# A decoder layer on one core: the three small slabs stored in order of the contraction, loaded and split in halves, with products of zeros on TensorE ahead of them

## The chip, the cores and the metric

The kernel runs on one core of one Trainium2 chip. The metric is the device time of one execution in microseconds (us). The core has five engines that run beside each other: TensorE (PE, matmuls; its weight loads are listed as PEld), VectorE (DVE), ScalarE (ACT), GpSimd (POOL) and SyncE (SP, here only the issuer of DMAs). They wait for each other through semaphores.

## The reference

One hybrid decoder layer on x of shape 256 x 2048 in float32. One input projection feeds 16 RWKV-7 heads and 8 heads of differential attention; an output projection, a layer norm, a squared-ReLU MLP (8192 wide) and a second layer norm follow.

```python
proj = x @ w_in[l]                     # 2048 x (3*1024 + 64 + 64 + 160 + 3*1024)
p = proj[..., :RWKV_COLS]
mixed = p + (_token_shift(p) - p) * mu # every column of the RWKV part
r, k, v, w_d, a_d, g_d = jnp.split(mixed, splits, axis=-1)
w = -jax.nn.softplus(-(w0 + jnp.tanh(w_d) @ w_up)) - 0.5
decay = jnp.exp(-jnp.exp(w))
a = jax.nn.sigmoid(a0 + a_d @ a_up)
g = jax.nn.sigmoid(g_d) @ g_up
...                                    # the scan over 256 steps, the attention
mix = jnp.concatenate([y_rwkv, y_diff], axis=-1) @ w_out[l]
x = _layer_norm(DEEPNORM_ALPHA * x + mix, ln1_gain[l], ln1_bias[l])
h = jnp.square(jax.nn.relu(x @ w_ff1[l])) @ w_ff2[l]
x = _layer_norm(DEEPNORM_ALPHA * x + h, ln2_gain[l], ln2_bias[l])
```

The change concerns the 288 small columns w_d, a_d and g_d of the first product, which need the most steps before anything else can use them: w_d (64 columns) and a_d (64) fill one accumulator of 128 columns, g_d (160) the next two, of which the second overlaps the first by 96 columns.

## The kernel before, in words

All weights reach the core in slabs of 128 partitions x 2048 float32 (1 MB). A slab lands in one of four `stage` buffers. ScalarE copies it to `whi` (rounded to fp32r), VectorE writes the rest, `stage - whi`, to `wlo`; there are two buffers of each. The activations are split in the same way into `acthi` and `actlo`. A product is then three fp32r matmuls: `whi*acthi`, `whi*actlo`, `wlo*acthi`, for each block of 128 columns (fb) and each block k of 128 of the 16 blocks of the contraction. The helper `mm` (L436) issues every matmul, so that nearly all TensorE rows have that line; they are told apart by their tiles. Likewise L1001 is every ScalarE operation, L1296 every full `wlo`, L1305 every `actlo`, L354 every slab's DMA.

The order of the work is written out by hand, in one program for each engine. The start goes as follows.

- SyncE issues x piece 0 (4 of 16 blocks, 512 KB), slab 0, x pieces 1 to 3, slab 1, two small vectors, slab 2, the weights `w_up` and `a_up`, the constants, slab 3 and the positions (L365 to L377). Later slabs wait for `lo_ready` of the slab that held their stage buffer.
- Slabs 0 and 1 together hold the columns of accumulators 0 and 1: slab 0 their first 8 blocks of the contraction, slab 1 the other 8. Slab 2 holds accumulator 2, all 16 blocks. TensorE therefore runs `chunk(0, 0, 0, ...)` over slabs 0 and 1, 96 matmuls, and then `chunk(2, 2, 2, ...)` over slab 2, 48 matmuls (L495, L496).
- After slab 1 (`slab_used` at 2) ScalarE copies accumulators 0 and 1 out of PSUM with a scale (L1028, L1029), VectorE adds the shifted term (`mix`, L1320, L1321), ScalarE takes the tanh of w_d (L1032). After slab 2 accumulator 2 gets the same (L1034, L1324).
- TensorE then multiplies tanh(w_d) by `wup` (four matmuls of full fp32, L504; they wait for the tanh, `lora_activated`), `aup` by `wa` (eight, L513) and the sums over time (sixteen, L516), with ScalarE's sigmoids and exponentials between them. These are fp32 tiles, not fp32r. From slab 3 on the main projection follows (L520 on).

Of the kernel before, what the change touches and what calls it, by code (L numbers as in the profile page):

```python
# [8 lines left out]
ALU = mybir.AluOpType  # L9
ACT = mybir.ActivationFunctionType  # L10
# [95 lines left out]
def build(nc, t):  # L106

    ctx = ExitStack()
    with ctx:
# [3 lines left out]
        def at(name, slot, shape, dtype=F32, byte=0):  # L113
            return nc.alloc_sbuf_tensor_at(name, shape, dtype, offset=BASE + slot * SL_BYTES + byte)
# [4 lines left out]
        def sem(name):  # L119
            return ctx.enter_context(nc.semaphore(name))  # L120
# [96 lines left out]

        s_stage = [sem(f"stage_loaded{i}") for i in range(NST)]
        s_hi, s_lo, s_used = sem("hi_ready"), sem("lo_ready"), sem("slab_used")
        s_free, s_mix = sem("acc_free"), sem("mix_scaled")  # L220
        s_x = [sem(f"x_loaded{i}") for i in range(4)]
        s_xhi, s_xlo = sem("act_hi_ready"), sem("act_lo_ready")
# [51 lines left out]
        def col(v, n=0):  # L274
            return vec[:, v + n:v + n + 1]
# [73 lines left out]
        def _(sp):  # L349
            def slab(n, k, src):  # L350

                if not (isinstance(n, int) and n < NST):
                    sp.wait_ge(s_lo, n - (NST - 1))
                sp.dma_start(stage[k % NST][:, :], src).then_inc(s_stage[k % NST], 16)  # L354
# [7 lines left out]
            def x_piece(j):  # L362
                sp.dma_start(xstage[:, 4 * j:4 * j + 4, :], t["xT"][:, 4 * j:4 * j + 4, :]).then_inc(s_x[j], 16)

            x_piece(0)  # L365
            slab(0, 0, t["w_in"][0])
            for j in range(1, 4):
                x_piece(j)
            slab(1, 1, t["w_in"][1])
            sp.dma_start(vec[:, 0:V_IN], t["vecs"]).then_inc(s_vecl, 16)  # L370
            sp.dma_start(lncol[:, :, :], t["ln1_cols"]).then_inc(s_lncol, 16)
            slab(2, 2, t["w_in"][2])
            sp.dma_start(wup[:, :], t["w_up"]).then_inc(s_lup, 16)
            sp.dma_start(aup[64:128, :], t["a_up"]).then_inc(s_lup, 16)
            sp.dma_start(cst[:, :], t["consts"][:, 0:C_SMALL]).then_inc(s_cst, 16)
# [58 lines left out]
        def _(pe):  # L434
# [18 lines left out]
                            last = both(b0 + fb, (k0 + s) % NHL, slice(256 * j + fb * P, 256 * j + fb * P + P), 8 * s + j)  # L453
                    last.then_inc(s_used, 1)

            def chunk(b0, g, k0, width=256, slabs=2, ready=None):


                kts = SLAB // width
                for s in range(slabs):  # L460
                    w = (k0 + s) % NHL
                    halves_ready(g + s)
                    for j in range(kts):
                        k = s * kts + j
                        if ready and k % 4 == 0:
                            pe.wait_ge(ready[0], ready[1] + k // 4)
                        for fb in range(width // P):
                            acc = ps[:, b0 + fb, 0:S]
                            cols = slice(j * width + fb * P, j * width + fb * P + P)
                            mm(acc, whi[w][:, cols], acthi[:, k, :], start=(k == 0), stop=False)  # L470
                            mm(acc, whi[w][:, cols], actlo[:, k, :], start=False, stop=False)
                            last = mm(acc, wlo[w][:, cols], acthi[:, k, :], start=False, stop=(k == KT - 1))
                    last.then_inc(s_used, 1)
# [18 lines left out]
                last.then_inc(s_used, 1)  # L492


            chunk(0, 0, 0, ready=(s_xlo, 1))  # L495
            chunk(2, 2, 2, width=128, slabs=1)  # L496

            pe.wait_ge(s_cst, 16)
            pe.wait_ge(s_lup, 32)
# [499 lines left out]
        def _(act):  # L999
            def A(out, in_, func, **kw):  # L1000
                return act.activation(out, in_, func, **kw)  # L1001
# [13 lines left out]
            def x_hi(j):  # L1015
                act.wait_ge(s_x[j], 16)
                A(acthi[:, 4 * j:4 * j + 4, :], xstage[:, 4 * j:4 * j + 4, :], ACT.Copy).then_inc(s_xhi, 1)

            x_hi(0)
            hi(0, 0)  # L1020
            for j in range(1, 4):
                x_hi(j)
            hi(1, 1)
            hi(2, 2)

            act.wait_ge(s_vec, 1)
            act.wait_ge(s_used, 2)
            A(wa[:, :], ps[:, 0, 0:S], ACT.Copy, scale=col(V_OMMU, 24))  # L1028
            A(sg[0][:, :], ps[:, 1, 0:S], ACT.Copy, scale=col(V_OMMU, 25)).then_inc(s_mix, 1)  # L1029
            hi(3, 3)  # L1030
            act.wait_ge(s_free, 1)
            A(wt[0:64, :], wa[0:64, :], ACT.Tanh).then_inc(s_lora, 1)  # L1032
            act.wait_ge(s_used, 3)
            A(sg[1][:, :], ps[:, 2, 0:S], ACT.Copy, scale=col(V_OMMU, 26)).then_inc(s_mix, 1)  # L1034
            A(sg[0][:, :], sg[0][:, :], ACT.Sigmoid).then_inc(s_lora, 1)
            act.wait_ge(s_free, 2)
            A(sg[1][:, :], sg[1][:, :], ACT.Sigmoid).then_inc(s_lora, 1)
# [250 lines left out]
        def _(dve):  # L1288
# [14 lines left out]
            def x_lo(j):  # L1303
                dve.wait_ge(s_xhi, j + 1)
                TTn(actlo[:, 4 * j:4 * j + 4, :], xstage[:, 4 * j:4 * j + 4, :], f(acthi[:, 4 * j:4 * j + 4, :]),  # L1305
                    ALU.subtract).then_inc(s_xlo, 1)

            dve.memset(wt[64:65, :], 1.0)
            x_lo(0)
            lo(0, 0)  # L1310
            for j in range(1, 4):
                x_lo(j)
            lo(1, 1)
            dve.wait_ge(s_vecl, 16)
            TS(vec[:, V_OMMU:V_OMMU + 27], vec[:, V_MU:V_MU + 27], -1.0, 1.0, ALU.mult, ALU.add)
            TS(vec[:, V_OMKA:V_OMKA + 8], vec[:, V_KA:V_KA + 8], -1.0, 1.0, ALU.mult, ALU.add)
            TS(vec[:, V_G08:V_G08 + 1], vec[:, V_SG:V_SG + 1], 1.0 - LAMBDA_INIT, None, ALU.mult).then_inc(s_vec, 1)
            lo(2, 2)
            dve.wait_ge(s_mix, 1)
            mix(wa, ps[:, 0, :], col(V_MU, 24))  # L1320
            mix(sg[0], ps[:, 1, :], col(V_MU, 25)).then_inc(s_free, 1)  # L1321
            lo(3, 3)
            dve.wait_ge(s_mix, 2)
            mix(sg[1], ps[:, 2, :], col(V_MU, 26)).then_inc(s_free, 1)  # L1324

# [453 lines left out]
def layout(inputs):  # L1779

    a = {k: np.asarray(v) for k, v in inputs.items()}
    w_in = a["w_in"][0]

    def cut(w, c0, width, slabs):

        piece = w[:, c0:c0 + width].reshape(slabs, KT // slabs, P, width)
        return piece.transpose(0, 2, 1, 3).reshape(slabs, P, -1)

    slabs = [cut(w_in, 3 * RW, 256, 2), cut(w_in, RCOLS - P, P, 1)]
    for j in range(RW // 256):  # L1790
        slabs += [cut(w_in, base + 256 * j, 256, 2) for base in (RW, 0, 2 * RW)]
        slabs += [cut(w_in, RCOLS + 256 * n, 256, 2) for n in (2 * j, 2 * j + 1)]
    slabs += [cut(w_in, RCOLS + 2 * RW + 512 * j, 512, 4) for j in range(2)]
    ff1 = np.concatenate([cut(a["w_ff1"][0], 256 * j, 256, 2) for j in range(N_FF1)])

    def blocks(v):
        return np.asarray(v).reshape(-1, P).T

    mu = a["mu_shift"][0]
    inv_freq = np.float32(10000.0) ** (-np.arange(0, HD, 2, dtype=np.float32) / np.float32(HD))  # L1800
    vecs = np.concatenate([
        blocks(mu[RW:2 * RW]), blocks(mu[0:RW]), blocks(mu[2 * RW:3 * RW]),
        blocks(mu[3 * RW:3 * RW + 2 * P]), blocks(mu[RCOLS - P:RCOLS]),
        blocks(a["rwkv_k_k"][0]), blocks(a["rwkv_k_a"][0]), blocks(a["rwkv_r_k"][0].reshape(-1)),
        blocks(a["rwkv_a0"][0]), blocks(a["rwkv_gn_gain"][0]), blocks(a["rwkv_gn_bias"][0]),
        a["diff_subln_gain"][0].reshape(P, 1),
        np.tile(inv_freq, 4).reshape(P, 1).astype(np.float32),
        np.tile(np.repeat(np.array([-1.0, 1.0], np.float32), 32), 2).reshape(P, 1),
        np.full((P, 1), GN_EPS, np.float32), np.full((P, 1), SUB_EPS, np.float32),
        np.full((P, 1), LN_EPS, np.float32)], axis=1)  # L1810
# [19 lines left out]
    return {k: np.ascontiguousarray(v) for k, v in out.items()}  # L1830
# [14 lines left out]
```

## Time and profile before

| what | value |
|---|---|
| runs, median of 3 | 1324.88 us (1322.53 to 1327.79) |
| the profiled execution | 1319.59 us |
| its span | 1317.7 us |
| mean granted TensorE clock | 0.991 |
| PE busy | 1265.3 us (96%) |
| DVE busy | 744.7 us (57%) |
| ACT busy | 568.8 us (43%) |
| DMA | 222.01 MB, mean 168 GB/s |

The span is the time from the first to the last record of the profiled execution; 1.89 us of its time lie outside. Busy time counts instructions at work. Matmuls overlap in the records: the time that one takes from the stream is the distance between starts, not the duration that is shown. A matmul of full fp32 is one call of `mm`, and two records in the profile.

### The profile page before, as it was taken

Reading aid. Unit: us, or ns where it says so; the run is one execution under the profiler, and the core shown is the slowest. Engines: PE = TensorE matmul, PEld = TensorE weight load, DVE = VectorE, ACT = ScalarE, POOL = GpSimd, SP = SyncE. Lnnn points to the kernel's source line nnn. Section 1 sums busy time; section 2 is a strip of 40 time slices with the busy share of each in tenths; the row PEclk is TensorE's granted clock in tenths of the full one; section 3 lists DMA queues with packets and bytes.
Section 4 is the critical chain, followed back from the end, with each engine's and each line's share of the span. In section 5 each row is a group of like instructions: output and inputs, shape, how many; then the busy total and the mean of one; then the engine's idle time right before and its main releaser. Section 6 shows DMA issues by size and latency. Waiting matters only on the chain.

```text
span 1317.7 us, 24390 instructions
## 1 busy us (share of the span) xinstructions
PE 1265.3 (96%) x10200; PEld 1101.1 (84%) x10200; DVE 744.7 (57%) x758; ACT 568.8 (43%) x615; POOL 85.2 (6%) x53
## 2 busy tenths in 40 slices
PE   6999999999999889989999999999999999999995
PEld 6899999987798767877888888888888888888884
DVE  5366757577633235677555555555555555655557
ACT  5644444456434223454333333333444444444443
POOL 0001202020000010019300000000000000000000
PEclk9999999999999999999999999999999999999998
DMA  8255454543100244563555555555565555555541
GB/s 340 98 181 189 163 191 161 188 165 135 37 4 3 93 170 134 195 246 130 193 190 190 189 191 191 191 191 191 191 255 190 191 190 192 192 192 191 191 159 64
DMA packets 33238, 222.01 MB, mean 168 GB/s; under 512 B 4725, under 2 KB 5109, under 8 KB 6926
## 3 DMA queue, kind: packets, MB, share of 16 engines
q1 hardware_dynamic: 33166, 220.94, 47.7%
q8 instruction: 59, 0.97, 0.3%
q14 instruction: 13, 0.11, 0.0%
HBM read 218.83 MB, written 2.10 MB: 168 GB/s over the span
## 4 chain that ended last, share of the span: by engine, by line
PE 88%; DVE 6%; ACT 3%; issue 2%; DMA 0%; SPq 0%; DVEq 0%; ACTq 0%
PE ps L436 88%; DVE wlo L1296 2%; ACT whi L1001 1%; PE ps L699 1%; DVE x1f L1645 0%; DMA stage<-w_in 0%; DVE stats L1610 0%; DVE xres L1715 0%; DVE xres L1609 0%; DVE xres L1713 0%; DVE rot L1419 0%; ACT L1001 0%; ACT xres L1001 0%; ACT kr L1001 0%; DVE yt L1568 0%
## 5 line engine op out<-in xcount | busy, mean ns | idle before, releaser
L1296 DVE TENSOR_TENSOR wlo<-stage,whi 128x2048 fp32r<-128x2048 f32 x192 | 450.8, 2348 | 435.0 <-ACT whi L1001 434.3
L1001 ACT ACTIVATE whi<-stage 128x2048 fp32r<-128x2048 f32 x194 | 371.8, 1916 | 606.3 <-PE ps L436 603.4
L436 PE MATMUL ps<-acts,whi 128*128 128x256 f32 (+1 forms) x2400 | 609.4, 332 | 17.0 <-DVE wlo L1296 15.1
L436 PE MATMUL ps<-acts,wlo 128*128 128x256 f32 x1712 | 482.0, 282 | 0.0
L436 PEld LDWEIGHTS ps<-acts,whi 128*128 128x128 f32 x2400 | 407.8, 190 | 64.9 <-issue 21.4
L436 PEld LDWEIGHTS ps<-acts,wlo 128*128 128x128 f32 x1712 | 326.2, 191 | 0.0
L436 PE MATMUL ps<-whi,shi 128*128 128x512 f32 x632 | 249.1, 394 | 2.8 <-DVE slo L1582 2.7
L436 PE MATMUL ps<-wlo,shi 128*128 128x512 f32 x632 | 247.7, 392 | 0.0
L436 PE MATMUL ps<-whi,slo 128*128 128x512 f32 x632 | 247.4, 391 | 0.0
L436 PEld LDWEIGHTS ps<-whi,shi 128*128 128x128 f32 x632 | 119.4, 189 | 35.8 <-issue 6.8
L436 PEld LDWEIGHTS ps<-wlo,shi 128*128 128x128 f32 x632 | 119.3, 189 | 25.6
L436 PEld LDWEIGHTS ps<-whi,slo 128*128 128x128 f32 x632 | 119.4, 189 | 23.2
L1582 DVE TENSOR_TENSOR slo<-hid,shi 128x512 fp32r<-128x512 f32 x64 | 43.8, 685 | 0.0
L436 PE MATMUL ps<-whi,acts 128*128 128x512 f32 x128 | 41.1, 402 | 0.2 <-DVE wlo L1296 0.2
L1001 ACT ACTIVATE shi<-hid 128x512 fp32r (+1 forms) x64 | 39.2, 613 | 1.1 <-PE ps L436 1.1
L436 PE MATMUL ps<-TT,XM 64*64 64x64 f32 x640 | 36.8, 218 | 0.0
L436 PEld LDWEIGHTS ps<-TT,XM 64*64 64x64 f32 x640 | 35.1, 135 | 0.0
L436 PE MATMUL ps<-XM,TT 64*64 64x64 f32 x512 | 32.8, 218 | 0.0
L1502 DVE TENSOR_TENSOR XM<-ps,levc 128x512 f32<-128x512 f32 x20 | 13.8, 692 | 32.9 <-PE ps L436 32.9
L436 PEld LDWEIGHTS ps<-XM,TT 64*64 64x64 f32 x512 | 31.3, 135 | 0.1
L436 PEld LDWEIGHTS ps<-whi,acts 128*128 128x128 f32 x128 | 22.9, 188 | 7.2 <-issue 3.1
L436 PE MATMUL ps<-wlo,acts 128*128 128x512 f32 x64 | 25.1, 392 | 0.0
(206 smaller groups left out, 838.5 us busy)
## 6 DMA issues: line engine op xcount, KB each, us to landing
stage<-w_ff SPq DMA_DIRECT2D x128, 1024.0 KB, 4.8
stage<-w_in SPq DMA_DIRECT2D x51, 1024.0 KB, 4.9
stage<-w_out SPq DMA_DIRECT2D x16, 1024.0 KB, 4.9
xstage<-xT SPq DMA_DIRECT2D x4, 512.0 KB, 6.9
xres<-x SPq DMA_DIRECT2D x1, 2048.0 KB, 7.7
gain<-ln_gain SPq DMA_DIRECT2D x2, 1024.0 KB, 7.5
bias<-ln_bias SPq DMA_DIRECT2D x2, 1024.0 KB, 9.6
out<-xres SPq DMA_DIRECT2D x8, 256.0 KB, 2.2
```

The lines of the kernel that those rows point to most:

```text
L436: return pe.matmul(out, lhsT, rhs, start=start, stop=stop, skip_group_check=True)
L699: last = pe.transpose(ps[:, n % 6, o:o + P], TURNED_SRC[n // 4](2 * (n % 4) + b2, a), ID)
L1001: return act.activation(out, in_, func, **kw)
L1296: TTn(wlo[k0 % NHL][:, :], stage[k0 % NST][:, :], f(whi[k0 % NHL][:, :]), ALU.subtract).then_inc(s_lo, 1)
L1502: TTn(by_head(XM), ab, over8(levc[:, lev, :]), ALU.mult).then_inc(s_xm, 1)
L1582: TTn(slo[h][:, :, :], src, f(shi[h][:, :, :]), ALU.subtract).then_inc(s_alo, 1)
```

## The change

The three small slabs hold the same 288 (with the overlap 384) columns, but in order of the contraction: block k of all three accumulators, then block k + 1. `layout` puts them so. Slab 0 thus holds k = 0 to 5 (the last in part), slab 1 up to 10, slab 2 the rest. Each is loaded by two DMAs of 128 x 1024 and split by two instructions on ScalarE and two on VectorE (`hi_half`, `lo_half`). SyncE issues the halves and the x pieces alternately, and the two small vectors after slab 2. TensorE runs one loop over 48 pairs of (k, fb), three matmuls each; all three accumulators end with slab 2. The copies out of PSUM therefore all stand behind slab 2, and the split of slab 3 stands ahead of them. VectorE first writes zeros to a tile of 128 x 384 float32, and TensorE starts with 18 matmuls on it, into bank 7 of PSUM, which nothing reads.

```diff
+WARM = 18
...
+        zeros = at("zeros", 13, [P, 3 * P])
...
+            def half_slabs(n):
+                sp.dma_start(stage[n][:, 0:SLAB // 2], t["w_in"][n][:, 0:SLAB // 2]).then_inc(s_half[n], 16)
+                sp.dma_start(stage[n][:, SLAB // 2:SLAB], t["w_in"][n][:, SLAB // 2:SLAB]).then_inc(s_stage[n], 16)
+
             x_piece(0)
-            slab(0, 0, t["w_in"][0])
-            for j in range(1, 4):
-                x_piece(j)
-            slab(1, 1, t["w_in"][1])
+            half_slabs(0)
+            x_piece(1)
+            half_slabs(1)
+            x_piece(2)
+            x_piece(3)
+            half_slabs(2)
             sp.dma_start(vec[:, 0:V_IN], t["vecs"]).then_inc(s_vecl, 16)
             sp.dma_start(lncol[:, :, :], t["ln1_cols"]).then_inc(s_lncol, 16)
-            slab(2, 2, t["w_in"][2])
...
-            chunk(0, 0, 0, ready=(s_xlo, 1))
-            chunk(2, 2, 2, width=128, slabs=1)
+            pe.wait_ge(s_zero, 1)
+            for _ in range(WARM):
+                mm(ps[:, 7, 0:2 * P], zeros[:, 0:P], zeros[:, P:3 * P])
+            for n in range(16 * N_LORA):
+                g, j = divmod(n, 16)
+                k, fb = divmod(n, 3)
+                if j == 0:
+                    pe.wait_ge(s_hih, g + 1)
+                    pe.wait_ge(s_loh, g + 1)
+                if j == 8:
+                    halves_ready(g)
+                if k % 4 == 0 and fb == 0:
+                    pe.wait_ge(s_xlo, k // 4 + 1)
+                w, cols, acc = g % NHL, slice(P * j, P * j + P), ps[:, fb, 0:S]
+                mm(acc, whi[w][:, cols], acthi[:, k, :], start=(k == 0), stop=False)
+                mm(acc, whi[w][:, cols], actlo[:, k, :], start=False, stop=False)
+                last = mm(acc, wlo[w][:, cols], acthi[:, k, :], start=False, stop=(k == KT - 1))
+                if j == 15:
+                    last.then_inc(s_used, 1)
...
+            def hi_half(n, part):
+                act.wait_ge((s_half, s_stage)[part][n], 16)
+                if n == 2:
+                    act.wait_ge(s_used, 1)
+                cols = slice(SLAB // 2 * part, SLAB // 2 * part + SLAB // 2)
+                A(whi[n % NHL][:, cols], stage[n][:, cols], ACT.Copy).then_inc((s_hih, s_hi)[part], 1)
...
             act.wait_ge(s_vec, 1)
-            act.wait_ge(s_used, 2)
+            act.wait_ge(s_used, 3)
             A(wa[:, :], ps[:, 0, 0:S], ACT.Copy, scale=col(V_OMMU, 24))
             A(sg[0][:, :], ps[:, 1, 0:S], ACT.Copy, scale=col(V_OMMU, 25)).then_inc(s_mix, 1)
-            hi(3, 3)
+            A(sg[1][:, :], ps[:, 2, 0:S], ACT.Copy, scale=col(V_OMMU, 26)).then_inc(s_mix, 1)
             act.wait_ge(s_free, 1)
             A(wt[0:64, :], wa[0:64, :], ACT.Tanh).then_inc(s_lora, 1)
-            act.wait_ge(s_used, 3)
-            A(sg[1][:, :], ps[:, 2, 0:S], ACT.Copy, scale=col(V_OMMU, 26)).then_inc(s_mix, 1)
...
+            dve.memset(zeros[:, :], 0.0).then_inc(s_zero, 1)
             dve.memset(wt[64:65, :], 1.0)
             x_lo(0)
-            lo(0, 0)
...
+            lo_half(0, 0)
+            lo_half(0, 1)
...
-    slabs = [cut(w_in, 3 * RW, 256, 2), cut(w_in, RCOLS - P, P, 1)]
+    lora = np.concatenate([w_in[:, 3 * RW:3 * RW + 256], w_in[:, RCOLS - P:RCOLS]], axis=1)
+    slabs = [lora.reshape(KT, P, 3 * P).transpose(1, 0, 2).reshape(P, N_LORA, SLAB).transpose(1, 0, 2)]
```

The start of TensorE's program before (a row: line of the kernel, operation, tile written and tiles read with buffer numbers, the shape of the instruction's moving side, the semaphores waited for, a count):

```order
L436 MATMUL ps<-acts_57,whi0_53 128x256 [waits act_lo_ready,lo_ready,hi_ready]
L436 MATMUL ps<-acts_57,whi0_53 128x256
L436 MATMUL ps<-acts_57,wlo0_55 128x256
L436 MATMUL ps<-acts_57,whi0_53 128x256 x2
L436 MATMUL ps<-acts_57,wlo0_55 128x256
```

The same place with the change:

```order
L445 MATMUL ps<-zeros_58 128x256 [waits zeros_written]
L445 MATMUL ps<-zeros_58 128x256 x17
L445 MATMUL ps<-acts_57,whi0_53 128x256 [waits act_lo_ready,half_lo_ready,half_hi_ready]
L445 MATMUL ps<-acts_57,whi0_53 128x256
L445 MATMUL ps<-acts_57,wlo0_55 128x256
L445 MATMUL ps<-acts_57,whi0_53 128x256 x2
L445 MATMUL ps<-acts_57,wlo0_55 128x256
L445 MATMUL ps<-acts_57,whi0_53 128x256 x2
```

The first real matmul now stands behind 18 products of `zeros`, and waits for the first half of the split of slab 0 in place of the whole.

ScalarE's program before, from the split of slab 0 to the tanh (`wt`) and the last copy out of PSUM (`sg` number 139):

```order
L1001 ACTIVATE whi0_53<-stage0_49 128x2048 [waits stage_loaded0]
L1001 ACTIVATE acts_57<-xstage_67 128x4x256 [waits x_loaded1]
L1001 ACTIVATE acts_57<-xstage_67 128x4x256 [waits x_loaded2]
L1001 ACTIVATE acts_57<-xstage_67 128x4x256 [waits x_loaded3]
L1001 ACTIVATE whi1_54<-stage1_50 128x2048 [waits stage_loaded1]
L1001 ACTIVATE whi0_53<-stage2_51 128x2048 [waits slab_used,stage_loaded2]
L1001 ACTIVATE wa_137<-ps,vec_135 128x256 [waits slab_used,vectors_ready]
L1001 ACTIVATE sg0_138<-ps,vec_135 128x256
L1001 ACTIVATE whi1_54<-stage3_52 128x2048 [waits slab_used,stage_loaded3]
L1001 ACTIVATE wt_136<-wa_137 64x256 [waits acc_free]
L1001 ACTIVATE sg1_139<-ps,vec_135 128x256 [waits slab_used]
```

With the change, from the last x piece to the sigmoids:

```order
L1023 ACTIVATE acts_57<-xstage_68 128x4x256 [waits x_loaded3]
L1023 ACTIVATE whi0_53<-stage2_51 128x1024 [waits slab_used,half_slab_loaded2]
L1023 ACTIVATE whi0_53<-stage2_51 128x1024 [waits slab_used,stage_loaded2]
L1023 ACTIVATE whi1_54<-stage3_52 128x2048 [waits slab_used,stage_loaded3]
L1023 ACTIVATE wa_138<-ps,vec_136 128x256 [waits slab_used,vectors_ready]
L1023 ACTIVATE sg0_139<-ps,vec_136 128x256
L1023 ACTIVATE sg1_140<-ps,vec_136 128x256
L1023 ACTIVATE wt_137<-wa_138 64x256 [waits acc_free]
L1023 ACT_TABLE_LOAD
L1023 ACTIVATE sg0_139<-sg0_139 128x256
L1023 ACTIVATE sg1_140<-sg1_140 128x256 [waits acc_free]
L1023 ACTIVATE sig_61<-ps 128x512 [waits decay_logits] x4
```

The copies `wa` and `sg` and the tanh, which stood between the splits of slabs 2 and 3 and waited for slab 1 alone, now stand behind the split of slab 3 and wait for the last small matmul.

## Rows read from the trace of the kernel before

**Rows 1.** The page: the chain of work that ended last (part 4).

```profile
PE 88%; DVE 6%; ACT 3%; issue 2%; DMA 0%; SPq 0%; DVEq 0%; ACTq 0%
```

**Rows 2.** Chain of waits in order of time, first 90 us: start, us, what (the 144 and the next 306 matmuls).

```profile
11.26 19.04 PE ps L436 x144
...
51.94 38.15 PE ps L436 x306
```

**Rows 3.** ScalarE in order of time: start, us, engine, line, operation, tiles, count [idle before].

```profile
4.46 1.06 ACT L1001 ACTIVATE acts<-xstage 128x1024 fp32r<-128x1024 f32 x1 [2.44 <-DMA xstage<-xT]
6.92 1.91 ACT L1001 ACTIVATE whi<-stage 128x2048 fp32r<-128x2048 f32 x1 [1.40 <-DMA stage<-w_in]
8.73 3.08 ACT L1001 ACTIVATE acts<-xstage 128x1024 fp32r<-128x1024 f32 x3
...
24.62 0.47 ACT L1001 ACTIVATE wa<-ps,vec 128x256 f32<-128x256 f32 x1 [3.84 <-PE ps L436]
25.00 0.47 ACT L1001 ACTIVATE sg<-ps,vec 128x256 f32<-128x256 f32 x1
...
27.15 0.41 ACT L1001 ACTIVATE wt<-wa 64x256 f32<-64x256 f32 x1
...
30.81 1.28 ACT L1001 ACT_TABLE_LOAD   x1
32.11 0.72 ACT L1001 ACTIVATE sg<-sg 128x256 f32<-128x256 f32 x2
32.74 2.04 ACT L1001 ACTIVATE sig<-ps 128x512 f32<-128x512 f32 x4
```

**Rows 4.** VectorE in order of time, the same columns.

```profile
0.86 0.27 DVE L1308 MEMSET wt<- 1x256 f32 x1 [0.86 <-PEq L1837]
5.55 1.23 DVE L1305 TENSOR_TENSOR acts<-xstage,acts 128x1024 fp32r<-128x1024 f32 x1 [4.42 <-ACT acts L1001]
8.86 2.29 DVE L1296 TENSOR_TENSOR wlo<-stage,whi 128x2048 fp32r<-128x2048 f32 x1 [2.08 <-ACT whi L1001]
...
25.50 0.48 DVE L1301 SCALAR_TENSOR_TENSOR wa<-ps,vec,wa 128x255 f32<-128x255 f32 x1 [2.39 <-ACT sg L1001]
25.90 0.47 DVE L1301 SCALAR_TENSOR_TENSOR sg<-ps,vec,sg 128x255 f32<-128x255 f32 x1
```

**Rows 5.** TensorE in order of time, its third and sixth matmul.

```profile
11.82 0.41 PE L436 MATMUL ps<-acts,wlo 128*128 128x256 f32 x1
...
12.46 0.41 PE L436 MATMUL ps<-acts,wlo 128*128 128x256 f32 x1
```

**Rows 6.** TensorE in order of time, later in the same stage.

```profile
18.12 0.28 PE L436 MATMUL ps<-acts,wlo 128*128 128x256 f32 x1
...
18.48 0.28 PE L436 MATMUL ps<-acts,wlo 128*128 128x256 f32 x1
```

**Rows 7.** Stretches: span: us, busy and count by engine, granted clock, DMA share, GB/s.

```profile
11.26:14.59 3.33, 3.33 (x15) 3.33 (x16) 3.30 (x3) 1.84 (x2) 0.00 (x0) 1.00 1.03 416
50.22:51.94 1.72, 0.00 (x0) 0.03 (x1) 1.57 (x1) 1.63 (x1) 0.00 (x0) 1.00 0.00 0
499.30:502.70 3.40, 0.71 (x4) 0.38 (x3) 3.40 (x4) 2.43 (x2) 0.00 (x0) 1.00 0.00 0
502.70:506.11 3.41, 3.41 (x10) 2.70 (x9) 2.31 (x2) 0.00 (x0) 0.00 (x0) 0.52 0.97 317
```

**Rows 8.** TensorE in order of time, matmuls of full fp32 tiles.

```profile
30.12 3.60 PE L436 MATMUL ps<-wup,wt 65*128 65x512 f32 x8
33.65 3.72 PE L436 MATMUL ps<-wa,aup 64*128 64x256 f32 x16
37.30 7.17 PE L436 MATMUL ps<-cst,sig 128*128 128x256 f32 x32
```

**Rows 9.** TensorE in order of time, from 503 us.

```profile
503.29 0.63 PE L436 MATMUL ps<-whi,shi 128*128 128x512 f32 x1
503.71 0.63 PE L436 MATMUL ps<-whi,slo 128*128 128x512 f32 x1
```

More of the change, by code:

```diff
@@ L219, in build @@
         s_hi, s_lo, s_used = sem("hi_ready"), sem("lo_ready"), sem("slab_used")
+        s_half = [sem(f"half_slab_loaded{i}") for i in range(N_LORA)]
+        s_hih, s_loh, s_zero = sem("half_hi_ready"), sem("half_lo_ready"), sem("zeros_written")
         s_free, s_mix = sem("acc_free"), sem("mix_scaled")
@@ L454, in pairs, with chunk @@
                     last.then_inc(s_used, 1)
-            def chunk(b0, g, k0, width=256, slabs=2, ready=None):
-                kts = SLAB // width
-                for s in range(slabs):
+            def chunk(b0, g, k0):
+                for s in range(2):
                     w = (k0 + s) % NHL
                     halves_ready(g + s)
[L463 to L467, printed above, removed]
+                    for j in range(8):
+                        k = s * 8 + j
+                        for fb in range(2):
                             acc = ps[:, b0 + fb, 0:S]
-                            cols = slice(j * width + fb * P, j * width + fb * P + P)
+                            cols = slice(256 * j + fb * P, 256 * j + fb * P + P)
                             mm(acc, whi[w][:, cols], acthi[:, k, :], start=(k == 0), stop=False)
@@ L1017, in x_hi @@
                 A(acthi[:, 4 * j:4 * j + 4, :], xstage[:, 4 * j:4 * j + 4, :], ACT.Copy).then_inc(s_xhi, 1)
-            x_hi(0)
[L1020 to L1024, printed above, removed]
+            def hi_half(n, part):
[4 more added lines that the diff above has]
+                A(whi[n % NHL][:, cols], stage[n][:, cols], ACT.Copy).then_inc((s_hih, s_hi)[part], 1)
+            x_hi(0)
+            hi_half(0, 0)
+            hi_half(0, 1)
+            x_hi(1)
+            hi_half(1, 0)
+            hi_half(1, 1)
+            x_hi(2)
+            x_hi(3)
+            hi_half(2, 0)
+            hi_half(2, 1)
+            hi(3, 3)
             act.wait_ge(s_vec, 1)
-            act.wait_ge(s_used, 2)
+            act.wait_ge(s_used, 3)
             A(wa[:, :], ps[:, 0, 0:S], ACT.Copy, scale=col(V_OMMU, 24))
             A(sg[0][:, :], ps[:, 1, 0:S], ACT.Copy, scale=col(V_OMMU, 25)).then_inc(s_mix, 1)
-            hi(3, 3)
+            A(sg[1][:, :], ps[:, 2, 0:S], ACT.Copy, scale=col(V_OMMU, 26)).then_inc(s_mix, 1)
             act.wait_ge(s_free, 1)
             A(wt[0:64, :], wa[0:64, :], ACT.Tanh).then_inc(s_lora, 1)
-            act.wait_ge(s_used, 3)
-            A(sg[1][:, :], ps[:, 2, 0:S], ACT.Copy, scale=col(V_OMMU, 26)).then_inc(s_mix, 1)
             A(sg[0][:, :], sg[0][:, :], ACT.Sigmoid).then_inc(s_lora, 1)
@@ L1306, in x_lo, with lo_half @@
                     ALU.subtract).then_inc(s_xlo, 1)
+            def lo_half(n, part):
+                dve.wait_ge((s_hih, s_hi)[part], n + 1)
+                if n == 2:
+                    dve.wait_ge(s_used, 1)
+                cols = slice(SLAB // 2 * part, SLAB // 2 * part + SLAB // 2)
+                TTn(wlo[n % NHL][:, cols], stage[n][:, cols], f(whi[n % NHL][:, cols]), ALU.subtract
+                    ).then_inc((s_loh, s_lo)[part], 1)
+            dve.memset(zeros[:, :], 0.0).then_inc(s_zero, 1)
             dve.memset(wt[64:65, :], 1.0)
             x_lo(0)
-            lo(0, 0)
-            for j in range(1, 4):
-                x_lo(j)
-            lo(1, 1)
+            lo_half(0, 0)
+            lo_half(0, 1)
+            x_lo(1)
+            lo_half(1, 0)
+            lo_half(1, 1)
+            x_lo(2)
+            x_lo(3)
+            lo_half(2, 0)
+            lo_half(2, 1)
             dve.wait_ge(s_vecl, 16)
@@ L1317, in _ @@
             TS(vec[:, V_G08:V_G08 + 1], vec[:, V_SG:V_SG + 1], 1.0 - LAMBDA_INIT, None, ALU.mult).then_inc(s_vec, 1)
-            lo(2, 2)
+            lo(3, 3)
             dve.wait_ge(s_mix, 1)
@@ L1321, in _ @@
             mix(sg[0], ps[:, 1, :], col(V_MU, 25)).then_inc(s_free, 1)
-            lo(3, 3)
             dve.wait_ge(s_mix, 2)
```

## The prediction

> **What bounds the kernel now.** I read the page's chain of work first: 88% of the span goes through TensorE, 6% through VectorE, 3% through ScalarE [rows 1]. TensorE is the bound nearly everywhere, so the change can only be worth what it does to the moments in which TensorE has nothing to do, or does it slowly, at the start. I read the chain in order of time next: TensorE begins the 144 small matmuls at 11.26 us and later the second slab of the main projection at 51.94 us, from where it runs on [rows 2]. Whatever moves 51.94 moves the end by as much, since behind it TensorE is fed in time. Then ScalarE and VectorE in order of time: x piece 0 lands at 4.46, slab 0 at 6.92, its split ends at 11.15 (8.86 + 2.29), and TensorE starts 0.11 later [rows 3, 4].
>
> TensorE's clock has two levels, 1.2 and 2.4 GHz. In the first 3.33 us of matmuls there are 15 [rows 7]; the third and the sixth start 0.64 apart, 0.213 for each, which is 256 columns at 1.2 GHz [rows 5]. Later three take 0.36, 0.12 for each [rows 6]. The granted-clock column says 1.00 in both stretches; I go by the spacing. The 144 take 15 x 0.213 + 129 x 0.12 = 18.7 us and end, as their successor on TensorE starts at 30.12 [rows 8], at F = 30.1. What counts below is when the `wup` products start, which is 30.12 before; all that follows is tied to them.
>
> **The halves and their order.** 1 MB takes 6.92 - 4.46 = 2.46 us behind x piece 0, so the first half of slab 0 lands at about 5.7. ScalarE splits it when the x copy is through (5.52): a 128x1024 copy takes 1.06, so it ends at 6.75. VectorE's x piece ends at 6.78, its half of `wlo` is as large and takes 1.23, so it ends at 8.0, and TensorE could start at 8.1, 3.1 us earlier than before [rows 3, 4]. I bound the half's landing by 5.7 and by 6.92 (as if it landed with the whole slab); the latter would give a start of 9.3. From there TensorE is not short of work: a half slab is 8 x 0.36 = 2.9 us of it, VectorE splits a half in 1.23 and an x piece in 1.23, nine more pieces at most, all done by about 19, and the DMA brings 0.5 MB in 1.3 us at 416 GB/s [rows 7]. Ten DMAs for x and the three slabs instead of seven cost SyncE issue time, which the transfers cover. The order of the contraction changes no count: 144 matmuls stay. Slab 3's split is moved ahead of the copies; it needs slab 1 done, 16 x 0.36 = 5.8 us before F', and takes 1.91 on ScalarE and 2.3 on VectorE, so it ends 1.5 us before F' and costs nothing.
>
> **The zeros.** They are float32, not fp32r. The trace shows what such a call costs: the 4 calls on `wup` are 8 records, the 16 on `cst` are 32 records in 7.17 us, 0.224 for each record of 256 columns, near two times 256 columns at 2.4 GHz [rows 8]. So 18 calls are 36 records, 36 x 0.224 = 8.1 us at 2.4 GHz. At 1.2 GHz a record of 256 columns passed twice should take what one of 512 columns takes there, 0.42 [rows 9]. VectorE starts its first instruction at 0.86 and takes 0.27 for 256 elements [rows 4]; for 384 I take 0.4, so TensorE starts at about 1.3. If it is slow for the first 3.33 us, as it was from 11.26 on [rows 7], that is 8 records, and the other 28 take 6.3: the zeros end at 1.3 + 3.3 + 6.3 = 10.9. Bounds: at 2.4 GHz from the first on 1.3 + 8.1 = 9.4; at 1.2 GHz to the last 1.3 + 36 x 0.42 = 16.4. I take 10.9, since the one start that the trace shows is the nearest row. So the zeros, not the loads, set when the real work begins: 2.8 us of the 3.1 are given back, and what they buy is that the 144 run at 2.4 GHz from the first on, 15 x (0.213 - 0.12) = 1.4 us. The real work starts at 11.0 and ends at F' = 11.0 + 144 x 0.12 = 28.3, 1.8 earlier than before.
>
> The Trainium skill, page "TensorE: Matmul & The Clock Gate", section "Part 1: The HAM clock gate", says that the slow clock is the default, that activity releases it, and that the point is "run-variable": one kernel showed 6, 11 or 14 slow matmuls. By its figures, as an estimate, the zeros would end between 10.6 and 12.2 here. The trace has one start only and cannot show the spread.
>
> **The wait that is new.** Before, the copies of accumulators 0 and 1, the two `mix` and the tanh lay under slab 2's matmuls: the tanh ended at 27.56, 2.6 ahead of the `wup` products that need it [rows 3, 8]. With all three accumulators ending together nothing covers them. Counted from F': the copy out of PSUM starts at about +0.2, the second 0.38 later (24.62 and 25.00) and ends at +1.05; VectorE's two `mix`, 25.50 to 26.37 in the trace, take 0.87 and end at +1.95; the tanh takes 0.41; with hand-overs `wup` starts at +2.5 [rows 3, 4]. Queued behind it on TensorE are the eight `aup` and the sixteen `cst` calls, which run without a gap before (30.12, 33.65, 37.30 [rows 8]), so the whole of 2.5 us passes on. ScalarE does not become later still: its table load (1.28) and the two sigmoids (0.72) end at about F' + 4.4, and the fourth `wup` product at F' + 6.0, where before they lay at 32.8 and 33.7 [rows 3, 8]. The stall of 1.72 us ahead of 51.94 [rows 7] hides none of it, since it is ScalarE's own chain behind the last `cst` product and moves along. Bounds of this term: 0, if something behind it has room that I do not see, and 2.5 plus the fall of the clock priced below.
>
> Sum: `wup` at 28.3 + 2.5 = 30.8 against 30.1, +0.7 us. On the profiled execution that is 1319.59 + 0.7 = 1320.3; the runs' median stands 5.3 higher, at 1324.88, and the same step gives 1325.5. No change can be told from under 0.5% (6.6 us) in measurements of this kernel; the runs alone span 5.3 us.
>
> **Rivals.**
> - The zeros are cheaper than fp32 rows say, one pass each: 18 x 0.213 = 3.8, over at 5.1. Then the loads decide: a start at 8.1. The 3 us idle before it may bring the slow clock back. F' is 8.1 + 17.3 = 25.4, or 26.8 with 15 slow matmuls, `wup` at 27.9 to 29.3: -2.2 to -0.8, about 1323.4. Against it: every call on float32 tiles in the rows has two records.
> - The clock falls in the new wait; this one is slower than before. In 499.30:502.70 TensorE was busy 0.71 of 3.40 us, and in the next 3.41 the granted clock is 0.52, 1.2 GHz; after 1.72 us idle at 50.22 no such stretch follows [rows 7]. A wait of 2.5 lies between. The price: in 3.41 us 8 records of 0.42 instead of 15 of 0.224, 7 x 0.224 = 1.6 us, all on the path, because the `wup` products are what runs slowly. It gives +2.3, 1327.2. It decides if the granted clock falls behind this wait as it did at 502.70, and not if it holds as at 51.94. The same page of the skill warns of idle gaps that return the clock to the slow level; the two rows agree with it in kind.
> - The zeros run at 1.2 GHz much longer than 3.33 us: at the bound of 16.4 the real work starts at 16.5 and `wup` at 36.3, +6.2, 1331. For it speaks only that the trace holds no zeros on TensorE.
> - The wait costs nothing behind all: -1.8, 1323.1. Against it stands the gapless TensorE from 30.12 on.
>
> **Chances.** Forecast (+0.7, between 0 and +1.5) 0.62; cheap zeros 0.13; clock falls in the wait 0.15; long slow zeros 0.06; wait without cost 0.04. All five lie within 6.6 us, so beyond 0.5% there is only the scatter of the measurement or something that no row shows: 0.04 on either side, 0.92 between. The range: the cases but for the last part of the slow zeros span 1322.7 to 1328; the medians of three runs have a scatter of their own of some 2 us (1322.53 to 1327.79), and I add it: 1320.5 to 1330.
>
> **What would show it.** Right: 36 records on `zeros` from about 1.3 to about 11; the first real matmul within 0.2 us of the last of them, with the split of the first half long over at 8.0; a spacing of 0.12 from the first real matmul on; no idle inside the 144; an idle stretch of 2.4 us before the `wup` products, ended by the tanh; `wup` near 30.8 and the second main slab near 52.6. Wrong: 18 records, or zeros over by 6; TensorE waiting for a `wlo` half among the 144; granted clock 0.52 behind the wait; the step at `wup` not found again at 51.94; or a difference that arises behind 60 us, where the two programs are the same.

## The result and the profile after

| | median us | lowest to highest | runs |
|---|---|---|---|
| before, with the change's runs | 1326.34 | 1322.53 to 1328.25 | 4 |
| with the change | 1338.49 | 1336.9 to 1344.53 | 4 |

The ratio is 1.0097 (95% interval 1.0062 to 1.0132): 12 us slower. The forecast was no change, +0.7 us, with a range of 1320.5 to 1330 us; the measured time lies above it. The profiled execution took 1338.66 us, its span is 1336.9 and its mean granted clock 0.978, against 1317.7 and 0.991 before.

I read the start first, in the order of the prediction's points. TensorE without the 144 small matmuls, in order of time (start, us, engine, line, operation, tiles, count):

```profile
1.33 9.64 PE L445 MATMUL ps<-zeros 128*128 128x256 f32 x36 [1.33 <-DVE zeros L1348]
...
31.44 6.70 PE L445 MATMUL ps<-wup,wt 65*128 65x512 f32 x8 [3.21 <-ACT wt L1023]
38.08 7.19 PE L445 MATMUL ps<-wa,aup 64*128 64x256 f32 x16
45.20 9.03 PE L445 MATMUL ps<-cst,sig 128*128 128x256 f32 x32
```

The zeros are 36 records from 1.33, as forecast; the first real matmul starts at 10.62 (forecast 11.0). The next two rows answer to [rows 8]: `wup` takes 6.70 in place of 3.60, `aup` 7.19 in place of 3.72. ScalarE and then VectorE at the same place:

```profile
7.22 1.06 ACT L1023 ACTIVATE whi<-stage 128x1024 fp32r<-128x1024 f32 x1 [1.59 <-DMA stage<-w_in]
...
25.71 1.92 ACT L1023 ACTIVATE whi<-stage 128x2048 fp32r<-128x2048 f32 x1 [5.34 <-DMA stage<-w_in]
28.33 0.47 ACT L1023 ACTIVATE wa<-ps,vec 128x256 f32<-128x256 f32 x1 [0.70 <-PE ps L445]
28.70 0.83 ACT L1023 ACTIVATE sg<-ps,vec 128x256 f32<-128x256 f32 x2
30.77 0.42 ACT L1023 ACTIVATE wt<-wa 64x256 f32<-64x256 f32 x1 [1.24 <-DVE sg L1333]
```

```profile
0.89 0.38 DVE L1348 MEMSET zeros<- 128x384 f32 x1 [0.89 <-PEq L1883]
...
27.66 2.29 DVE L1328 TENSOR_TENSOR wlo<-stage,whi 128x2048 fp32r<-128x2048 f32 x1 [5.80 <-ACT whi L1023]
29.87 0.47 DVE L1333 SCALAR_TENSOR_TENSOR wa<-ps,vec,wa 128x255 f32<-128x255 f32 x1
```

The tanh, `wt`, ends at 31.19, 3.0 us after the last small matmul, which ends 3.21 ahead of `wup`, at 28.23. Stretches of the changed kernel (span: us, then busy and count of PE, PEld, DVE, ACT, POOL, granted clock, DMA share, GB/s):

```profile
11.00:28.10 17.10, 17.10 (x144) 17.03 (x142) 9.12 (x11) 8.28 (x7) 0.00 (x0) 1.00 1.03 367
28.10:31.44 3.34, 0.13 (x2) 0.03 (x1) 3.31 (x6) 1.85 (x5) 0.00 (x0) 1.00 0.99 390
31.44:38.08 6.64, 6.64 (x9) 2.27 (x9) 3.15 (x9) 3.45 (x6) 0.00 (x0) 0.54 0.42 162
38.08:45.20 7.12, 7.12 (x17) 5.17 (x17) 0.00 (x0) 3.91 (x8) 0.00 (x0) 0.50 0.00 0
45.20:49.00 3.80, 3.80 (x10) 3.08 (x10) 0.00 (x0) 2.63 (x4) 0.00 (x0) 0.50 0.01 4
49.00:54.20 5.20, 5.20 (x26) 4.59 (x26) 0.00 (x0) 5.13 (x12) 0.00 (x0) 1.00 0.00 0
```

The 144 run from 10.62 to 28.2 without idle time, at 0.12 each. In the gap behind them, 3.2 us, TensorE does nothing. Behind it the granted clock is 0.54, 0.50 and 0.50, that is 1.2 GHz, through `wup`, `aup` and the first ten records on `cst`, and 1.00 after them. That is 17 us at half the clock. The two starts below answer to 30.12 [rows 8] and 51.94 [rows 2]; the rows are of the chain of waits:

```profile
31.44 18.48 PE ps L445 x36
...
61.65 28.43 PE ps L445 x230
```

The second main slab starts at 61.65 in place of 51.94, 9.7 us later. From there to the end the two programs are the same, yet the profiled pair differ by another 9.5 (19.2 in span). The medians differ by 12.2, so most of these 9.5 us needed an explanation of their own.

### The profile page after: what moved, and what is told of

Its sections match the earlier page's. It is cut to its first block, busy times and chain, and to the rows that moved or that the text cites. A ratio compares the mean times of both kernels' runs of the same rounds, so it can differ in the third digit from the quotient of the medians.

```text
span 1336.9 us, 24477 instructions
## 1 busy us (share of the span) xinstructions
PE 1288.4 (96%) x10236; PEld 1115.1 (83%) x10236; DVE 746.4 (56%) x762; ACT 571.6 (43%) x618; POOL 85.1 (6%) x53
## 4 chain that ended last, share of the span: by engine, by line
PE 88%; DVE 6%; ACT 2%; issue 2%; DMA 1%; SPq 1%; DVEq 0%; ACTq 0%
PE ps L445 87%; DVE wlo L1328 2%; DMA stage<-w_in 1%; ACT whi L1023 1%; PE ps L721 1%; DVE stats L1655 0%; DVE xres L1760 0%; DVE x1f L1690 0%; DVE xres L1654 0%; DVE xres L1758 0%; DVE rot L1464 0%; ACT xres L1023 0%; ACT kr L1023 0%; PE ps L574 0%; DVE qk L1463 0%
## 5 line engine op out<-in xcount | busy, mean ns | idle before, releaser
L1328 DVE TENSOR_TENSOR wlo<-stage,whi 128x2048 fp32r<-128x2048 f32 x189 | 443.8, 2348 | 436.4 <-ACT whi L1023 435.9
L1023 ACT ACTIVATE whi<-stage 128x2048 fp32r<-128x2048 f32 (+1 forms) x197 | 372.3, 1890 | 612.0 <-PE ps L445 602.1
```

The lines of the kernel that those rows point to most:

```text
L1328: TTn(wlo[k0 % NHL][:, :], stage[k0 % NST][:, :], f(whi[k0 % NHL][:, :]), ALU.subtract).then_inc(s_lo, 1)
```

## The experiments

Theory G: the gap before `wup` lets the clock fall, and the products on 65 and 64 rows behind it don't bring it back. Z, T and D are the rivals to it; each is stated in the expectation of the run that first tests it. In the table "start" is the start of the second main slab, in each kernel's trace; 51.94 before. The first four, the next four and e8 with before_again ran in three groups, each on one chip with the kernel before, whose median there stands beside theirs.

| kernel | start | shift of start | median, before's | ratio (95%) |
|---|---|---|---|---|
| e1_fill | 53.33 | +1.4 | 1330.48, 1328.76 | 1.0022 (0.9998 to 1.0046) |
| e2_wait_only | 61.55 | +9.6 | 1339.06, 1328.76 | 1.0084 (1.0051 to 1.0117) |
| e3_no_zeros | 59.87 | +7.9 | 1336.78, 1328.76 | 1.0058 (1.0024 to 1.0093) |
| e5_after_gap | 56.77 | +4.8 | 1332.88, 1328.76 | 1.0024 (1.0001 to 1.0046) |
| e7_full_rows | 54.38 | +2.4 | 1332.39, 1328.41 | 1.0035 (1.0013 to 1.0056) |
| after_again | 60.76 | +8.8 | 1340.31, 1328.41 | 1.0103 (1.0057 to 1.0149) |
| e4_halves | 51.11 | -0.8 | 1326.30, 1328.41 | 0.9991 (0.9970 to 1.0013) |
| e6_halves_zeros | 52.97 | +1.0 | 1327.85, 1328.41 | 0.9990 (0.9968 to 1.0012) |
| e8_split_halves | 49.45 | -2.5 | 1325.98, 1328.68 | 0.9980 (0.9958 to 1.0003) |

**The gap filled (e1_fill).**

```diff
+            for _ in range(8):
+                mm(ps[:, 7, 0:2 * P], zeros[:, 0:P], zeros[:, P:3 * P])
             pe.wait_ge(s_cst, 16)
             pe.wait_ge(s_lup, 32)
             pe.wait_ge(s_lora, 1)
```

> The changed kernel, with eight more products of zeros (16 records, 3.6 us at 2.4 GHz) between the last small matmul and the `wup` products, so that TensorE does not stand idle in the wait for the tanh. Theory G (the 3.2 us gap lets the clock fall, and the products on 65 and 64 rows behind it don't bring it back): the granted clock stays 1.00 through `wup`, `aup` and `cst`, `wup` starts near 31.9 and takes 3.6 in place of 6.7, the second main slab starts near 53.5 in place of 61.65, and the time is 8 us below the changed kernel's (1330 against 1338.5). Rival Z (the changed start itself, zeros or the phase in which the clock is decided, brings the slow stretch): the granted clock is about 0.5 behind 31 as before and the time stays at 1338 or above. Rival D (half of the loss arises behind 60 us for a reason of its own): the start is cured and the time falls by less than 8.

```profile
28.06 3.62 PE L445 MATMUL ps<-zeros 128*128 128x256 f32 x16
31.52 3.60 PE L445 MATMUL ps<-wup,wt 65*128 65x512 f32 x8
35.04 3.72 PE L445 MATMUL ps<-wa,aup 64*128 64x256 f32 x16
```

```profile
31.52:38.69 7.17, 7.17 (x25) 4.24 (x23) 2.74 (x8) 6.51 (x14) 0.00 (x0) 1.00 0.36 141
```

`wup` starts at the same moment as with the change, but takes 3.60 again, and the clock is 1.00. The start comes to 53.33 as G said, and the median is 1.7 us above the kernel before, where the changed kernel's is 12. Z falls. By D some 9 us would remain with the start cured; 1.7 does, with an interval of -0.3 to +6.1 us.

**The wait alone, in the kernel before (e2_wait_only).** VectorE's `lo(3, 3)` moves likewise.

```diff
             hi(2, 2)
+            hi(3, 3)
             act.wait_ge(s_vec, 1)
-            act.wait_ge(s_used, 2)
+            act.wait_ge(s_used, 3)
             A(wa[:, :], ps[:, 0, 0:S], ACT.Copy, scale=col(V_OMMU, 24))
             A(sg[0][:, :], ps[:, 1, 0:S], ACT.Copy, scale=col(V_OMMU, 25)).then_inc(s_mix, 1)
-            hi(3, 3)
+            A(sg[1][:, :], ps[:, 2, 0:S], ACT.Copy, scale=col(V_OMMU, 26)).then_inc(s_mix, 1)
```

> The kernel before, with one thing of the change: the copies of accumulators 0 and 1, their `mix` and the tanh stand behind slab 2, and the split of slab 3 ahead of them. No zeros, no halves, the old order of storage. Theory G: TensorE stands idle for 2.4 to 3.2 us before `wup`, the clock falls to 1.2 GHz, `wup` takes 6.7 and `aup` 7.2, the second main slab starts near 51.9 + 2.5 + 8 = 62.5, and the time is 10 to 12 us above the kernel before. Rival Z: the wait costs its own 2.5 us and no more, about 1328.5, granted clock 1.00 throughout.

```profile
33.05 4.61 PE L436 MATMUL ps<-wup,wt 65*128 65x512 f32 x8 [2.55 <-ACT wt L1001]
37.58 7.19 PE L436 MATMUL ps<-wa,aup 64*128 64x256 f32 x16
44.70 9.42 PE L436 MATMUL ps<-cst,sig 128*128 128x256 f32 x32
```

```profile
30.30:33.05 2.75, 0.20 (x3) 0.04 (x1) 1.55 (x5) 1.86 (x5) 0.00 (x0) 1.00 0.84 328
33.05:37.58 4.53, 4.53 (x8) 1.55 (x8) 3.15 (x9) 3.33 (x6) 0.00 (x0) 0.79 0.04 18
37.58:44.70 7.12, 7.12 (x17) 5.11 (x16) 0.00 (x0) 3.91 (x8) 0.00 (x0) 0.50 0.00 0
```

A gap of 2.55, the granted clock 0.79 and then 0.50, start 61.55, median 10.3 above. This one step makes the whole loss, without zeros, halves or the new order of storage. It is made up a little otherwise than with the change: `wup` starts 2.9 later than before, and from there to the second main slab 28.50 us pass, 6.7 more than the 21.82 before (8.4 more with the change).

**No zeros (e3_no_zeros).** `WARM = 0` and no wait for `s_zero` in the changed kernel.

> The changed kernel without the 18 products of zeros. The real work can start at 9.6, when the first half of slab 0 is split, and runs slowly for 3.4 us or more: the 144 end at 9.6 + 18.8 = 28.4, against 28.1 with the zeros. Theory G: the gap before `wup` is 3 us as before, the slow stretch comes again, the time is that of the changed kernel within 1 us (1338.5). Rival Z: without the zeros the slow stretch is gone and the time falls by 8 to 1330.

TensorE starts at 9.66, `wup` at 31.37 behind a gap of 2.55, and the slow stretch is there. The time is 8.0 above the kernel before; the zeros are not the cause. What they bring is small: `wup` starts at 31.37 without them; with them at 31.44 in the first trace, where slab 3 came late and the gap was 3.21, and at 30.56 in after_again, where the gap was 2.55 as here. At an equal gap that is 0.8 us.

**Full-array products behind the gap (e5_after_gap).** The same two lines as in e1, five times, behind the waits.

> The changed kernel with five products of zeros (10 records on the full array, 4.3 us at 1.2 GHz) behind the wait for the tanh and ahead of `wup`; the gap itself stays. Theory G says that a product on 128 rows brings the clock back and those on 65 and 64 rows don't: the granted clock is 0.5 for about 3.4 us and back at 1.00 before `wup` or within its first records, so 4.3 us are added and `wup`, `aup` and `cst` get back to about 14 us from 22.9; net 3 to 5 us below the changed kernel, about 1334.5. Rival T (once fallen here the clock stays low for some 17 us whatever runs): the slow stretch is as long as before and the time is 4.3 above the changed kernel, 1343.

```profile
31.02:34.07 3.05, 3.05 (x11) 2.54 (x12) 2.74 (x8) 1.77 (x3) 0.00 (x0) 0.73 0.74 301
34.07:38.47 4.40, 4.40 (x9) 1.65 (x7) 0.41 (x2) 1.79 (x3) 0.00 (x0) 0.80 0.00 0
38.47:42.12 3.65, 3.65 (x17) 2.91 (x17) 0.00 (x0) 3.51 (x8) 0.00 (x0) 1.00 0.01 4
```

The clock is 1.00 again when `aup` starts. By the shares the first two stretches hold 3.4 us at half the clock together, where the change had 17. The start is 4.9 us earlier than with the change, though 3.05 us of products were added. By rival T the stretch would be as long as before; T falls.

**All 128 rows (e7_full_rows).** SyncE waits for the first memset before it loads `wup[0:65]`, TensorE for both.

```diff
-                    mm(ps[:, bk, 0:S], aup[64:128, P * b:P * b + P], wa[64:128, :]).then_inc(s_item, 1)
+                    mm(ps[:, bk, 0:S], aup[:, P * b:P * b + P], wa[:, :]).then_inc(s_item, 1)
...
-            dve.memset(wt[64:65, :], 1.0)
+            dve.memset(wt[64:128, :], 1.0)
...
+            pool.memset(wup[64:128, :], 0.0).then_inc(s_pad, 1)
+            pool.memset(aup[0:64, :], 0.0).then_inc(s_pad, 1)
```

> The changed kernel with the `wup` and `aup` products on all 128 rows: the rows that were not used are filled with zeros (by GpSimd, at the start) and taken into the product, so that the sums are the same and each product takes as many columns as before. The gap of about 3 us before `wup` stays. Theory G (the clock falls in the gap, and products on 65 and 64 rows don't bring it back while those on 128 rows do): granted clock about 0.5 for 3.4 to 6.8 us and 1.00 before the `aup` products are through; the second main slab 6 us earlier than in the changed kernel, near 55.5, and the time 6 us below it. Rival T (once fallen, the clock comes back only some 14 to 17 us later whatever rows are used): the slow stretch is as long as with the change and the time is the same.

```profile
30.99 5.37 PE L447 MATMUL ps<-wup,wt 128*128 128x512 f32 x8 [2.55 <-ACT wt L1026]
36.19 3.62 PE L447 MATMUL ps<-wa,aup 128*128 128x256 f32 x16
39.65 7.07 PE L447 MATMUL ps<-cst,sig 128*128 128x256 f32 x32
```

```profile
30.99:36.19 5.20, 5.20 (x8) 2.18 (x9) 3.14 (x9) 3.44 (x6) 0.00 (x0) 0.67 0.51 197
36.19:39.65 3.46, 3.46 (x18) 3.04 (x17) 0.00 (x0) 3.26 (x8) 0.00 (x0) 1.00 0.00 0
```

The gap is the same (2.55), and so are count and columns of the records; only the rows differ: `wup` takes 5.37, `aup` 3.62, the start is at 54.38. T falls again. The median is 4.0 above the kernel before, the start 2.4; the changed kernel in the same group (after_again, 4 runs) is at 11.9 and 8.8. From the start of `wup` to the second main slab 23.39 us pass, 1.6 more than before. With the gap kept, the rows in use decide whether the fall costs 1.6 us or 6.7 to 8.4 (e2, e3, after, after_again).

**The changed kernel and the kernel before once more.**

> The changed kernel once more, on the chip of its neighbours here, so that its cost can be set beside theirs and its stretches at the lower clock behind 60 us be compared with the first trace. Theory G: 9 to 10 us above the kernel before, from the start alone; what stands behind 60 us differs from execution to execution and is no property of the change. Rival D (the change costs another 9 us behind 60 us, as the two first traces say): 18 or more above.

> The kernel before, traced once more. If what differs behind 60 us between the first two traces (9.4 us) belongs to the execution and not to the change, this trace has the same start as the first (second main slab at 51.9) and another sum behind it, by some 2 to 10 us; if it belongs to the change, the two traces of the kernel before agree within 1 us behind 60 us.

after_again: start 60.76, 11.9 above the kernel before; the gap is 2.55 this time and the stretch at 0.5 is there. before_again: start 52.16, and 1320.30 us in its one execution. Behind the start it differs from the first trace by 0.6 us only (spans 1318.5 and 1317.7, starts 52.16 and 51.94), where 2 to 10 were expected, so by the letter of what I had written the other 9 us would belong to the change. The stages say otherwise. A stretch in which nothing but the MLP's first product runs, in the first trace of before, then after, after_again and e1_fill:

```profile
700.00:900.00 200.00, 200.00 (x1155) 176.34 (x1155) 106.14 (x73) 77.66 (x54) 0.00 (x0) 1.00 0.54 189
```

```profile
700.00:900.00 200.00, 200.00 (x1156) 174.81 (x1155) 105.77 (x72) 78.00 (x55) 0.00 (x0) 1.00 0.54 189
```

```profile
700.00:900.00 200.00, 200.00 (x1134) 173.53 (x1133) 105.62 (x72) 75.66 (x53) 0.00 (x0) 1.00 0.53 185
```

```profile
700.00:900.00 200.00, 200.00 (x1135) 173.54 (x1134) 104.39 (x72) 75.81 (x53) 0.00 (x0) 1.00 0.53 184
```

TensorE is fully busy and at 1.00 in all, but does about 1155 or 1134 matmuls, 1.9% apart. Over that stage (from the first to the last copy into `hid`, 344 us) it makes 6.4 us. The traces of before, before_again, after, e4, e7 and e8 have the fast pace, those of after_again, e1, e2, e3, e5 and e6 the slow one: it goes with the execution and not with the change: the changed kernel has one pace in its first trace and the other in its second, and e2, which is the kernel before in that stage, has the slow one. The executions traced at the fast pace stand 5.9 to 8.4 us below the medians (before, before_again, e4, e7, e8), except the changed kernel's, 1338.66. What sets the pace I have not found. That first pair, though, has the same pace. Its difference behind the start (8.5 us by the first copy into `hid`, at 608 us before) goes with more stretches at the lower clock between 290 and 610 us: the mean there is 0.95 in after and 0.98 before (0.77 from 470 to 500 us of after). In after_again the difference by the same point is 2.0. Neither part was tested by an edit; that they are no property of the change rests on after_again and on the medians, whose shifts follow the start within 3.1 us in all nine rows of the table.

**Parts of the change that keep the cover (e4_halves, e6_halves_zeros, e8_split_halves).** In all three the storage is the old one, so slab 2 still covers the copies and the tanh. e4 and e6 load and split slabs 0 and 1 in halves, alternating with the x pieces (`half_slabs(0, 1)` is the first half of slab 0, x piece 1, the second half); e6 adds `WARM = 15`. e8 loads them whole and in the old order, splits them in halves (`act.wait_ge(s_stage[n], 16)` ahead of both), and has `WARM = 14`.

```diff
             x_piece(0)
-            slab(0, 0, t["w_in"][0])
-            for j in range(1, 4):
-                x_piece(j)
-            slab(1, 1, t["w_in"][1])
+            half_slabs(0, 1)
+            x_piece(2)
+            half_slabs(1, 3)
```

> The kernel before with slabs 0 and 1 loaded and split in halves, and nothing else of the change: the old order of storage, so slab 2's matmuls still cover the copies and the tanh, and no zeros. TensorE should start at 9.7 in place of 11.3, run the 144 without a wait, and reach `wup` at 28.5 without a gap, the second main slab at 50.3; granted clock 1.00 through `wup` and `aup`. The time is 1.6 us below the kernel before by theory G. A rival, that more and smaller transfers at the start cost as much as they bring, has it at the same time or above.

> The last one with 15 products of zeros ahead (30 records, over at 9.7, when the first half is split). The 144 run at 2.4 GHz from the first on and end at 27.1; no gap before `wup`; the second main slab at 49. By theory G 3 us below the kernel before, and the best of all. By rival Z (zeros themselves lead to a slow stretch later) there is a stretch at about 0.5 of the clock between 27 and 50 and the time is above the kernel before.

e4: TensorE starts at 9.37, `wup` at 29.29 without a gap, start 51.11; the median is 2.1 below, with an interval that takes in 1; `wup` and the start came 0.8 later than expected. e6 missed: TensorE waits 2.39 us at 21.4 for slab 2, which had landed at 19.4, and the clock falls again; the products behind that gap are on 128 rows and it is back within two stretches:

```profile
21.40:23.85 2.45, 0.06 (x2) 0.03 (x1) 2.44 (x2) 0.84 (x2) 0.00 (x0) 1.00 1.01 405
23.85:27.30 3.45, 3.45 (x21) 3.45 (x22) 0.66 (x3) 1.97 (x2) 0.00 (x0) 0.70 1.02 420
...
31.15:38.00 6.85, 6.85 (x25) 4.24 (x24) 3.91 (x11) 6.62 (x14) 0.00 (x0) 1.00 0.41 166
```

> The kernel before, with slabs 0 and 1 loaded whole and in the old order of DMAs, but split in halves on ScalarE and VectorE, and 14 products of zeros (28 records, over at about 9.1) ahead. The traces with halved loads show the DMA at 200 to 300 GB/s from 4 to 6 us where whole slabs have 400, and slab 2 landing at 19.4, which made TensorE wait 2.39 us there and let the clock fall. Theory: with whole loads slab 2 lands near 16, TensorE starts at 9.3 at 2.4 GHz, waits at most 0.5 us for slab 1, reaches `wup` at 27.2 without a gap and the second main slab at 49; no stretch at 0.5 of the clock before 290 us; 2.9 us (0.2%) below the kernel before, which 5 rounds may or may not resolve. Rival: the small waits inside the 144 bring the clock down again, and the second main slab stands at 51 or later.

```profile
1.33 9.20 PE L439 MATMUL ps<-zeros 128*128 128x256 f32 x28 [1.33 <-DVE zeros L1333]
...
27.64 3.60 PE L439 MATMUL ps<-wup,wt 65*128 65x512 f32 x8
31.16 3.72 PE L439 MATMUL ps<-wa,aup 64*128 64x256 f32 x16
```

```profile
3.50:6.00 2.50, 2.50 (x7) 1.96 (x7) 0.36 (x1) 1.06 (x1) 0.00 (x0) 1.00 1.00 416
```

The same stretch in the changed kernel:

```profile
3.50:6.00 2.50, 2.50 (x10) 2.08 (x10) 0.33 (x1) 1.06 (x1) 0.00 (x0) 1.00 0.93 243
```

The DMA moves 416 GB/s against 243. `wup` starts at 27.64, 2.5 us before that of the kernel before, with the clock at 1.00; the start is 49.45. The median is 2.7 us below (0.998), but the interval ends at 1.0003: better by the trace, not resolved by the times. It has the lowest ratio of all that I ran; its interval overlaps those of e4 and e6. The first real matmul starts at 10.18, where 9.3 was expected.

## Why the prediction was wrong

- **The zeros: right.** 36 records, start 1.33, the first real matmul at 10.62 (forecast 1.3 and 11.0), no slow matmul behind them.
- **The halves: the end was right, the way was not.** The first half was to land at 5.7; ScalarE could take it at 7.22, later than the whole slab 0 in the kernel before (6.92). Half-size loads at the start ran at 243 GB/s. The bound that I gave, 6.92, was the nearer end. It cost nothing on the path, since the zeros ended later still. Slab 3, though, which I had let wait for slab 1 only, landed at 25.7 behind them (24.3 in after_again); its `wlo` ended at 29.95 and held up `mix`.
- **The 144: right.** No wait among them, 28.1 against 28.3.
- **The wait: the mechanism right, the size 3.2 for 2.5,** by slab 3. In the other traces with a gap ahead of `wup` it is 2.55, behind the copies.
- **The clock behind the wait: here it failed.** I had this as a rival with a chance of 0.15 and a price of 1.6 us. The price was wrong and the chance too low. The price took for granted that the lower level lasts one stretch of 3.41 us, as at 502.70 [rows 7], where full-array products follow. Here products on 65 and 64 rows follow, and it lasted 17 us: `wup` +3.1, `aup` +3.5, `cst` +1.9, 8.4 in all between the starts of `wup` and of the second main slab (30.21 us against 21.82). With 28.2 + 3.2 - 30.1 = +1.3 ahead of it the sum is the measured +9.7. Where the same products use all rows (e7) the fall costs 1.6 us, the very price that I gave: it holds for products on the full array and not for those behind this gap. And the chance: all six traces with the gap of 2.55 to 3.21 here show the fall.
- **No change beyond the scatter: wrong by the same step.** I had put 0.04 on slower by more than 0.5%; it is 0.97%.
- **The cases were too narrow.** I took each price from a stretch with other work behind it, and so found that nothing could leave 6.6 us.

The length of a gap alone does not decide whether the clock falls. A gap of 2.76 us further on, ended by the same step in all twelve traces, is followed by a fall in five (after, e1, e3, e5, e6) and by no fall in the other seven. The first 3.41 us behind it in the kernel before, then in e1_fill:

```profile
346.99:350.40 3.41, 3.41 (x135) 3.00 (x135) 3.41 (x6) 1.15 (x3) 0.00 (x0) 1.00 0.02 5
348.31:351.72 3.41, 3.41 (x71) 2.88 (x71) 3.13 (x6) 0.49 (x1) 0.00 (x0) 0.65 0.02 5
```

What decides there was not tested, so how likely the fall at the start is beyond the traces with such a gap there stays open.

The Trainium skill, page "TensorE: Matmul & The Clock Gate", section "HAM oscillation — how this bites in real kernels", says that waits which leave the array idle let the clock fall and that the work behind them starts at the slow level. The seven traces with such a gap at the start agree in kind; by the granted clock of their stretches the fall came 0.5 us (after) to 2.6 us (e2) behind the gap's end, not at once. I had named the page beside the rival and gone by the milder row for its chance.

## What to carry to other kernels

A gap on TensorE is priced by what follows it. Ahead of products on half of the rows, a gap of 2.5 to 3.2 us cost 7 to 8 us more than itself; filling it with products that nothing reads, using all rows, or keeping independent matmuls over it took most of that back. Before reordering a contraction so that all sums end together, look what ran under the last of them.

## What the runs showed of the hardware

- Idle times of TensorE of 2.39 to 3.21 us between matmuls at 2.4 GHz, here ahead of 62 us, were followed by a granted clock of 0.5 in all seven traces that have one; the idle time of 1.7 us ahead of the second main slab (1.67 to 1.91 in all twelve) never was. Further on the same length went both ways: 1.95 to 1.98 us (at 291.47 us before) was followed by a fall in seven of twelve, 2.76 us (at 346.99) in five of twelve.
- Products on 65 and 64 rows for 7.2 us did not lower a clock of 1.00 (before, e1, e4, e8), and for 13 us did not raise one of 0.50 (after, after_again). Once products on 128 rows ran, it was at 1.00 5.2 us later at the latest (after, e7).
- One program's stage of dense matmuls ran at one of two paces, about 1155 or 1134 matmuls in 200 us, at a granted clock of 1.00 in both. The cause is open.
- Loads of 512 KB, 4 KB to a partition, at the start of the program: 243 GB/s from 3.5 to 6 us, where alternating with a 1 MB slab gave 416 (e8). The cause is open.
